# A YOCO-style decoder step on Trainium2: the eight experts of the MoE written out in a row instead of looped

## What is computed

```python
def moe_ffn(x, w_router, wg, wu, wd):
    B, T, D = x.shape
    xf = x.reshape(B * T, D)
    logits = (xf @ w_router).astype(jnp.float32)
    top_v, top_i = lax.top_k(logits, TOP_K_EXPERTS)
    top_w = jax.nn.softmax(top_v, axis=-1)
    combine = jnp.sum(jax.nn.one_hot(top_i, N_EXPERTS, dtype=jnp.float32) * top_w[..., None], axis=1)
    out = jnp.zeros_like(xf)
    for e in range(N_EXPERTS):
        out = out + combine[:, e:e + 1].astype(x.dtype) * swiglu(xf, wg[e], wu[e], wd[e])
    return out.reshape(B, T, D)
```

## Time and profile before

| what | value |
|---|---|
| median of 3 runs | 1921.69 us (1919.1 to 1922.94) |
| the profiled execution's own time | 1924.66 us |
| its span, first to last instruction | 1922.9 us |
| PE busy | 1765.7 us (92%), 19980 matmul records and as many weight loads |
| DVE, ACT, POOL busy | 386.6, 263.9, 138.0 us (20%, 14%, 7%) |
| DMA traffic | 486.13 MB, mean 253 GB/s |
| mean granted TensorE clock | 0.956 |
| first MoE matmul, last MoE matmul | 1034.09 us, 1893.06 us |

### The profile page before, as it was taken

One profiled execution on the slowest core, in us unless ns is written; L12 is line 12 of the kernel. 1 busy time (PEld: TensorE's weight loads), 2 busy tenths in 40 slices (PEclk: granted clock), 3 DMA queues, 4 the chain that ended last, 5 costly groups with the idle time before them and its releaser, 6 DMA issues.

```text
span 1922.9 us, 45150 instructions
## 1 busy us (share of the span) xinstructions
PE 1765.7 (92%) x19980; PEld 1316.5 (68%) x19980; DVE 386.6 (20%) x846; ACT 263.9 (14%) x588; POOL 138.0 (7%) x198
## 2 busy tenths in 40 slices
PE   6599999899999999998887999989899989999993
PEld 4488998677777777665676955545794545697552
DVE  2789002200000303665321000000000000000002
ACT  1001001100000113555302001001000101000011
POOL 2045000200000002034001000000000000000001
PEclk9799999899999898999887999989999999999997
DMA  9935566494483445579763999989889999999992
GB/s 241 248 98 170 182 210 225 152 368 142 140 318 132 125 111 187 207 250 334 185 217 117 313 340 309 378 291 379 284 307 343 339 368 294 376 322 336 307 373 94
DMA packets 356007, 486.13 MB, mean 253 GB/s; under 512 B 32768, under 2 KB 313226, under 8 KB 355176
## 3 DMA queue, kind: packets, MB, share of 16 engines
q1 hardware_dynamic: 325600, 392.40, 61.8%
q10 hardware_dynamic: 17096, 45.66, 7.3%
q0 software_dynamic: 13120, 45.15, 6.7%
HBM read 450.51 MB, written 40.98 MB: 256 GB/s over the span
## 4 chain that ended last, share of the span: by engine, by line
issue 46%; PE 46%; ACT 2%; DVE 2%; another core or an unknown queue 1%; DMA 1%; ACTq 1%; POOL 0%; SPq 0%; POOLq 0%; DVEq 0%
PE ps L1527 16%; PE ps L1557 8%; PE ps L1651 4%; PE ps L1673 2%; PE ps L1838 2%; PE ps L1696 2%; PE ps L1757 1%; PE ps L1849 1%; PE ps L1905 1%; PE ps L1495 1%; PE ps L1753 1%; ACT arena L926 1%; PE ps L1788 1%; PE ps L1770 1%
## 5 line engine op out<-in xcount | busy, mean ns | idle before, releaser
L1527 PE MATMUL ps<-arena 128*128 128x288 f32 x1216 | 304.5, 414 | 24.7 <-DMA arena<-in_conv_w_pw 19.6
L1527 PEld LDWEIGHTS ps<-arena 128*128 128x128 f32 x1216 | 235.5, 194 | 93.0 <-DMA arena<-in_conv_w_pw 18.7
L1988 PE MATMUL ps<-arena 128*128 128x128 f32 x2112 | 240.7, 277 | 7.3 <-issue 6.0
L1988 PEld LDWEIGHTS ps<-arena 128*128 128x128 f32 x2112 | 240.2, 194 | 8.5 <-issue 8.5
L2037 PE MATMUL ps<-arena 128*32 128x256 f32 x3520 | 207.2, 387 | 16.6 <-issue 16.6
L2037 PEld LDWEIGHTS ps<-arena 128*32 128x32 f32 x3520 | 116.8, 112 | 94.9 <-issue 25.8
L1557 PE MATMUL ps<-arena 64*64 64x128 f32 x4096 | 160.3, 313 | 5.3 <-issue 5.3
L1557 PEld LDWEIGHTS ps<-arena 64*64 64x64 f32 x4096 | 156.1, 248 | 9.2 <-issue 8.6
L2070 PE MATMUL ps<-arena 128*32 128x256 f32 x2640 | 144.6, 379 | 0.0
L1436 DVE TENSOR_TENSOR arena<-arena,ps 64x256 f32<-64x256 f32 (+2 forms) x55 | 30.7, 559 | 491.6 <-ACT arena L999 491.6
L2070 PEld LDWEIGHTS ps<-arena 128*32 128x32 f32 x2640 | 84.5, 109 | 56.4 <-issue 0.8
(11 more groups left out here) (348 smaller groups left out, 1338.6 us busy)
## 6 DMA issues: line engine op xcount, KB each, us to landing
arena<-in_moe_w_gate SPq DMA_DIRECT2D x88, 1024.0 KB, 11.4
arena<-in_moe_w_up SPq DMA_DIRECT2D x88, 1024.0 KB, 11.2
arena<-in_moe_w_down SPq DMA_DIRECT2D x88, 1024.0 KB, 10.6
arena<-in_cache_kv SPq DMA_DIRECT2D x176, 256.0 KB, 5.5
arena<-in_cache_kv POOLq DMA_DIRECT2D x80, 256.0 KB, 7.4
xg_scratch<-arena POOLq DMA_DIRECT2D x26, 512.0 KB, 17.8
arena<-in_conv_w_pw SPq DMA_DIRECT2D x12, 1024.0 KB, 15.3
arena<-in_cmp_w ACTq DMA_DIRECT2D x6, 2048.0 KB, 23.0
```

What stands on the lines that cost most here:

```text
L1527: ins = mm(dst, w[:, k, c * P:(c + 1) * P], rhs[:, k, :], start=(k == 0), stop=(k == KD - 1))
L1988: ins = mm(dst, w[:, k, c * P:(c + 1) * P], XeT[:, k, :], start=(k == 0), stop=(k == KD - 1))
```

## The change

The places' capacities become a table `CAPS` that has the same values as before, and what was worked out from `CAP` is now worked out from it. On PE, ACT and DVE the two loops become a Python loop over the eight places, so each engine's stream holds eight bodies one behind the other; `turn` and `n` become constants, and with them the values that semaphores are compared with. `fewer` gets a third argument, the number of groups of 32 rows; with these capacities it is always 3, so the branches for 2 are never built. The bodies' matmuls, activations and products, their shapes and their order stay. A new constant `places` (128 x 21 floats) holds ranks, row offsets and capacities of experts 1 to 7; it is one more DMA among ACT's table loads, and the waits for `in_att` go from 25 to 26 DMAs. DVE picks place and capacity from it by comparing each rank with the seven ranks, multiplying and summing, in place of the chain of comparisons.

```diff
-CAP = P - 32
-YZERO = 21 * 16
+CAPS = (128, 96, 96, 128, 96, 96, 128, 96)
+SMALL = [j for j in range(NE) if CAPS[j] < P]
+YZERO = (16 + len(SMALL)) * 16
+YPUT = [YZERO]
+for _c in CAPS:
+    YPUT.append(YPUT[-1] + 16 * (3 if _c == P else _c // 32))
...
+    others = sorted(range(1, NE), key=lambda j: (-CAPS[j], j))
+    ranks = np.concatenate([np.arange(NE - 1), [P * j for j in others], [CAPS[j] for j in others]])
+    c["places"] = np.broadcast_to(ranks[None], (P, 3 * (NE - 1)))
...
+        ranked = take(3, NE - 1)
...
-        HROW = [(4 if u % 2 else 3 if u == 10 else 2) * P for u in range(11)]
-        HCOL = [(384 * (u // 2) + 128 * (u % 2), 384 * (u // 2) + 128 * (u % 2) + HROW[u] // 2) for u in range(11)]
+
+        def hrow(ng, u):
+            return P * (2 if ng == 2 else 4 if u % 2 else 3 if u == 10 else 2)
+
+        def hcol(ng, u):
+            return 128 * u if ng == 2 else 384 * (u // 2) + 128 * (u % 2)
+
+        def y_before(turn):
+            return YPUT[turn] if isinstance(turn, int) else turn * 48 + (YPUT[NE] - 48 * NE)
...
-                              (before, "before"), (earl8, "earlier8"), (erow, "expert_row"), (edge, "rank_edge")]:
+                              (before, "before"), (earl8, "earlier8"), (erow, "expert_row"), (ranked.rearrange("p a b -> p (a b)"), "places"), (edge, "rank_edge")]:
                 act.dma_start(dst, a[name]).then_inc(sem("in_att"), 16)
...
-            for b in (1, 2, 4, 5, 7):
-                act.dma_start(yg_dram[b * P + CAP:(b + 1) * P, :], zero[0:P - CAP]).then_inc(sem("y_put"), 16)
+            for b in SMALL:
+                act.dma_start(yg_dram[b * P + CAPS[b]:(b + 1) * P, :], zero[0:P - CAPS[b]]).then_inc(sem("y_put"), 16)
...
-                act.wait_ge(sem("y_put"), turn * 48 + YZERO)
+                act.wait_ge(sem("y_put"), y_before(turn))
...
-            def fewer(n, turn):
+            def fewer(n, turn, ng):
...
-                    act.wait_ge(slot_used, turn * EPAD + (M0 + (2 * u + 2 if u % 2 or u == 10 else 2 * u + 1)))
+                    act.wait_ge(slot_used, turn * EPAD + (M0 + (2 * u + 1 if ng == 3 and u % 2 == 0 and u < 10 else 2 * u + 2)))
...
-            with act.Fori(0, 2, 1) as h:
-                experts(h * 3)
-                with act.Fori(0, 2, 1) as s:
-                    fewer(h * 2 + s, h * 3 + (s + 1))
-            experts(6)
-            fewer(4, 7)
+            for j in range(NE):
+                if CAPS[j] == P:
+                    experts(j)
+                else:
+                    fewer(SMALL.index(j), j, CAPS[j] // 32)
...
-            dve.wait_ge(sem("in_att"), 25 * 16)
+            dve.wait_ge(sem("in_att"), 26 * 16)
...
-            order = sort8[:, others, others]
-            link(v.tensor_tensor(order, key8[:, others].unsqueeze(1).to_broadcast([P, NE - 1, NE - 1]),
-                                 key8[:, others].unsqueeze(2).to_broadcast([P, NE - 1, NE - 1]), ALU.is_gt))
-            r7, c7, k7, first, second = (x[:, others] for x in (rank8, cap8, key8, place[:, 0], place[:, 1]))
-            link(v.tensor_reduce(r7, order, AXX, ALU.add))
-            v.tensor_scalar(c7, r7, 2.0, float(P - CAP), ALU.is_lt, ALU.mult)
-            v.tensor_scalar(second, r7, 0.0, 4.0, ALU.is_equal, ALU.mult)
-            v.tensor_scalar(k7, r7, 1.0, 6.0, ALU.is_equal, ALU.mult)
-            link(v.scalar_tensor_tensor(out=first, in0=r7, scalar=4.0, in1=r7, op0=ALU.is_ge, op1=ALU.add))
-            v.tensor_scalar(c7, c7, float(CAP), None, ALU.add)
-            v.tensor_tensor(k7, k7, second, ALU.add)
-            link(v.scalar_tensor_tensor(out=first, in0=r7, scalar=6.0, in1=first, op0=ALU.is_ge, op1=ALU.add))
+            order, key7 = sort8[:, others, others], key8[:, others]
+            link(v.tensor_tensor(order, key7.unsqueeze(1).to_broadcast([P, NE - 1, NE - 1]),
+                                 key7.unsqueeze(2).to_broadcast([P, NE - 1, NE - 1]), ALU.is_gt))
+            link(v.tensor_reduce(rank8[:, others], order, AXX, ALU.add))
+            link(v.tensor_tensor(order, rank8[:, others].unsqueeze(2).to_broadcast([P, NE - 1, NE - 1]),
+                                 ranked[:, 0].unsqueeze(1).to_broadcast([P, NE - 1, NE - 1]), ALU.is_equal))
+            picked = rkB.rearrange("p t a b -> p (t a b)")[:, 0:2 * (NE - 1) ** 2].rearrange("p (i a b) -> p i a b", i=2, a=NE - 1)
+            for i in range(2):
+                ins = v.tensor_tensor(picked[:, i], order, ranked[:, 1 + i].unsqueeze(1).to_broadcast([P, NE - 1, NE - 1]), ALU.mult)
+            link(ins)
+            v.tensor_reduce(cap8[:, others], picked[:, 1], AXX, ALU.add)
+            link(v.tensor_reduce(place[:, 1, others], picked[:, 0], AXX, ALU.add))
             v.tensor_scalar(room8, cap8, -1.0, float(NE * P), ALU.mult, ALU.add)
-            link(v.scalar_tensor_tensor(out=first, in0=first, scalar=-1.0, in1=k7, op0=ALU.add, op1=ALU.add))
             link(v.tensor_tensor(pfx, pfx, cap8.unsqueeze(1).to_broadcast([P, 3, NE]), ALU.subtract))
-            link(v.tensor_scalar(place[:, 1], place[:, 0], float(P), None, ALU.mult))
...
-            with dve.Fori(0, 2, 1) as h:
-                experts(h, h * 3)
-                with dve.Fori(0, 2, 1) as s:
-                    fewer(h * 2 + s, h * 3 + (s + 1))
-            experts(2, 6)
-            fewer(4, 7)
+            for j in range(NE):
+                if CAPS[j] == P:
+                    experts(j, j)
+                else:
+                    fewer(SMALL.index(j), j, CAPS[j] // 32)
...
-            pe.wait_ge(sem("in_att"), 25 * 16)
+            pe.wait_ge(sem("in_att"), 26 * 16)
...
-            with pe.Fori(0, 2, 1) as h:
-                experts(h * 3)
-                with pe.Fori(0, 2, 1) as s:
-                    fewer(h * 2 + s, h * 3 + (s + 1))
-            experts(6)
-            fewer(4, 7)
+            for j in range(NE):
+                if CAPS[j] == P:
+                    experts(j)
+                else:
+                    fewer(SMALL.index(j), j, CAPS[j] // 32)
```

More of the change, by code:

```diff
@@ L985, in experts @@
                     act.dma_start(yg_dram[bass.ds(turn * P + r0, n), :], Ye[r0:r0 + n, :]).then_inc(sem("y_put"), 16)
-            def fewer(n, turn):
+            def fewer(n, turn, ng):
                 def columns_in(u):
-                    c0, c1 = HCOL[u]
+                    c0, cn = hcol(ng, u), hrow(ng, u) // 2
                     act.wait_ge(sem("ht_mm"), n * 11 + (u + 1))
-                    sc.activation(HT[:, c0:c1], ps[:, 7, 64:64 + c1 - c0], ACT.Copy).then_inc(sem("ht_ev"), 1)
+                    sc.activation(HT[:, c0:c0 + cn], ps[:, 7, 64:64 + cn], ACT.Copy).then_inc(sem("ht_ev"), 1)
                 for u in range(11):
@@ L996, in fewer @@
                         columns_in(u - 1)
-                    act.wait_ge(slot_used, turn * EPAD + (M0 + (2 * u + 2 if u % 2 or u == 10 else 2 * u + 1)))
+                    act.wait_ge(slot_used, turn * EPAD + (M0 + (2 * u + 1 if ng == 3 and u % 2 == 0 and u < 10 else 2 * u + 2)))
                     act.wait_ge(sem("gu_ev"), turn * 11 + (u + 1))
-                    sc.activation(es[64:, u % 2, 0:HROW[u]], ps[0:64, 2 + u % 2, 0:HROW[u]], ACT.Silu)\
+                    sc.activation(es[64:, u % 2, 0:hrow(ng, u)], ps[0:64, 2 + u % 2, 0:hrow(ng, u)], ACT.Silu)\
                       .then_inc(sem("gu_exp"), 1)
@@ L1004, in fewer @@
                 act.wait_ge(slot_used, turn * EPAD + (M0 + 33))
-                act.wait_ge(sem("y_put"), turn * 48 + YZERO)
-                y = Ye[:, 0:3 * 256].rearrange("p (g c) -> p g c", g=3)
-                sc.activation(y, ps[:, 4:7, 0:256], ACT.Copy).then_inc(sem("y_ev"), 1)
+                act.wait_ge(sem("y_put"), y_before(turn))
+                y = Ye[:, 0:ng * 256].rearrange("p (g c) -> p g c", g=ng)
+                sc.activation(y, ps[:, 4:4 + ng, 0:256], ACT.Copy).then_inc(sem("y_ev"), 1)
                 act.wait_ge(sem("y_ev"), turn + 2)
-                for g in range(3):
+                for g in range(ng):
                     act.dma_start(yg_dram[bass.ds(turn * P + 32 * g, 32), :].rearrange("t (j c) -> j t c", j=4), y[:, g, :])\
                        .then_inc(sem("y_put"), 16)
-            with act.Fori(0, 2, 1) as h:
-                experts(h * 3)
-                with act.Fori(0, 2, 1) as s:
-                    fewer(h * 2 + s, h * 3 + (s + 1))
-            experts(6)
-            fewer(4, 7)
+            for j in range(NE):
[3 more added lines that the diff above has]
+                    fewer(SMALL.index(j), j, CAPS[j] // 32)
             act.wait_ge(sem("flag_ready"), 1)
@@ L1024, in _ @@
                         experts(r * NE + e)
-                act.wait_ge(sem("y_put"), YZERO + 3 * NE * 48)
+                act.wait_ge(sem("y_put"), YPUT[NE] + 2 * NE * 48)
                 act.wait_ge(sem("xe_in"), (3 * NE + 2) * 16)
-            act.wait_ge(sem("y_put"), YZERO + NE * 48)
+            act.wait_ge(sem("y_put"), YPUT[NE])
```

(24 more changed lines are left out.)

## The result

The changed kernel takes 1888.32 us (median of 4 runs, 1884.33 to 1891.38) against 1921.35 us of the kernel before (median of 4, the three of the table ahead among them): 33.0 us less. The ratio on record is 0.9837, 95% interval 0.9821 to 0.9853; it is not the quotient of the two medians (0.9828), and by it the gain is 31.3 us. Forecast were 30.8 us less and 1890.9 us. A second measurement gave 1889.51 against 1918.74 us, a ratio of 0.9848 (0.983 to 0.9866), 29.2 us less. The forecast gain lies between the two; the forecast time lies 1.4 to 2.6 us above both.

A forecast was written before the change was run, and what follows sets the result against it. PE bounds the eight turns, with 22.6 us of "issue" stops at loop jumps. Gains of 30.94 and 0.27 less 0.45 give 30.8 us, from the median 1921.69 to 1890.9 us; range 1887 to 1899.

The forecast's parts named there:

- PE without jumps: PE's three jumps back in the expert turns: removing them gains 30.94 us, 22.6 idle and 8.3 slow clock.
- What is late next: Rows, ACT and weights for turn 2, needed up to 12 us earlier, still come in time; no wait taken.
- The room of 3 to 5 us: Reserve of the last down-projection weight slots in turn 2: some 5 us, 3 with the rows' and results' megabyte.
- the rival on this: Weights come late in turns 2 and 5: 7 us for both pairs, 1898 us; chance 8%.
- ACT and DVE without loops: Their jumps lie under PE's matmuls, and they stand idle for PE in every step: nothing gained.
- The pick by table: DVE, from ranking to scatter: six linked steps for seven, gain 0.27 us, between 0.5 gain and 0.3 loss.
- the table's load: One more issue in ACT's table loads lengthens PE's wait behind them: loss 0.45 us, between 0 and 0.9.
- The stop is of the edge: Edges between turns, not jumps, stop PE, so the stops stay: 1921.9 us; chance 3%.
- The code itself becomes the bound: PE's code supply falls behind in straight turns; at 7.3 us a packet it costs 42 us, 1933 us; chance 3%.
- The sign at which the last matmul was to end: If the forecast is right, the last matmul of the eight turns ends near 1862.3 us.

The follow-up runs named there:

- PE alone: Kernel before with PE's eight turns written out, ACT and DVE keeping loops, ranking and tables as before: 1886.15 us, ratio 0.9844 to the kernel before.
- one loop put back: Changed kernel with PE running turns 1 and 2 as a loop of two trips, everything else written out: 1898.74 us, ratio 0.9899.
- one and three megabytes more: Changed kernel with SP copying one or three more megabytes in each of turns 1 to 7 into unread DRAM: 1886.22 and 1904.82 us.
- the table alone: Changed kernel with the loops of before on PE, ACT and DVE, keeping the table, its DMA and the picking: 1921.21 us, ratio 1.0011.
- the added loops: Changed kernel with loops of unused matmuls added on PE ahead of three turns: stops of 1.4 to 1.6 us at 1760, 2240 and 2560 instructions.

## Why the prediction was right

**PE without jumps** was the term that mattered, 30.94 us forecast and 31.37 measured over turns 1 to 7. Pricing each edge up to a mark behind the slow stretch, and not by the idle time alone, took in the slow clock: the 22.6 us of "issue" by themselves would have been more than a quarter short. That the stop belongs to the jump was read from the edges 2 to 3 and 5 to 6; the runs with PE alone and with one loop put back show it. Why a jump stops PE was no part of the forecast; the runs above show it.

**What is late next:** nothing, as forecast. PE waits for no weight in turns 2 and 5. The room of 3 to 5 us came out near enough, in part by luck. The working took the 343 GB/s of turn 1 for what DMA can give; turn 2 now moves 369, and turn 1 itself moved 353 and 369 GB/s with one and three megabytes more. And it looked for the tightest slot among the last of the down projection, where the trace has it at step 9, with 2.45 and 1.72 us to spare. (The sum of the rival on this reads 1342.6 us where 1268.3 + 74 is 1342.3; nothing hangs on it.)

**ACT and DVE without loops:** nothing, as forecast (ratio 1.0). **The pick by table and the table's load** came out at -0.21 and +0.45 us, too small for the medians to tell: the table alone has a ratio of 1.0011, whose interval takes in 1. Nor can PE's wait behind the list tell it: it was 5.33 us before and 7.2 after, but 6.9 and 7.0 us in the two kernels without the new table and 5.7 us with the table alone.

**The rivals.** "The stop is of the edge" fell with turns 2 and 5 of the changed kernel, which follow their 96-row turns without a stop. "The code itself becomes the bound" fell too: no piece of "issue" is left in the turns, with 78 packets of code in the 706.85 us of turns 1 to 7 (84 in 738.22 before).

**What the forecast did not have.** Turn 0 takes 119.3 us after (1026.16 to 1145.42) and took 120.7 before: the granted clock rises 3 us into the turn rather than 6. Turn 0 takes 119.2 to 119.3 us in each kernel of the study that has both the table and a turn 0 written out on PE, and 120.6 to 120.8 in the three that lack one or both. Why the clock rises earlier there is open; nothing was tried on it. It is 1.5 us of the 33. The sign at which the last matmul was to end, 1862 us, was set by the front part of one execution and is missed by 10 us, 8 of them before turn 0.

## What to carry to other kernels

Where an engine that bounds the kernel shows "issue" gaps at the places where a loop jumps back, price the jump from the end of one trip to where the next has caught up with a trip that had no stop, since slow clock can stand behind the idle time (0.50 behind the stop of 5.8 us here, 1.00 behind the one of 2.5 us). A loop whose body is short enough to stay at hand (1200 instructions here) can be left as it is; a longer one (1760 and more here) is worth writing out on the bounding engine alone, the more so while the DMA queues are full, and the loops of engines that wait anyway can stay. Before that, check that the transfers which the stop had covered still come in time without it.

## What the runs showed that was not expected

More than half of the stop behind a jump is owed to the full DMA queues: 5.8 us with the weights streaming, 2.5 us without, for the same jump and the same code on PE. The expectation of 5 to 6 us at the largest of the added loops failed on this.

Straight code has small stops too. In the compression of the cache pages, where PE has no loop, the page of the kernel after has this group (records, busy us and mean ns, idle us before them):

```profile
L1568 PE MATMUL ps<-arena 64*64 64x128 f32 x4096 | 158.9, 310 | 4.7 <-issue 4.7
```

Here 4096 records take 158.9 us, some 0.04 us each, against 0.055 in a turn of 96 rows (7.04 us for 128), so PE uses up its code faster; the 4.7 us of "issue" are six pieces. The trace says what they are: each of the six ends 1.35 to 1.52 us after a packet of code has ended, the same step as from the packet to the end of the branch behind a jump (1.4 to 1.6 us). So it is the code that comes late there; a run that changes its supply was not made.
